# A hybrid decoder step with expert retrieval on one core: mixer steps of the second and third groups laid closer, VectorE without a slot's lag

## The reference

```
h1  = rmsnorm(x) * (1 + sc1) + sh1
proj = h1 @ w_in + b_in                 # 1024 -> 1536: pooling part, conv value, conv gate
pool_out = (window means over 2/4/8/16 rows - hp) @ w_pool * pool_scale
conv_out = silu(layernorm(depthwise causal conv, 31 taps, of cv * sigmoid(cg)))
x  = x + gt1 * (concat(pool_out, conv_out) @ w_out + b_out)
h2 = rmsnorm(x) * (1 + sc2) + sh2
q  = h2 @ w_query                       # 1024 -> 2048 (8 heads, 2 halves of 128)
s  = q . sub_keys                       # 128 scores for each head and half
16 best of each half -> 256 sums -> 16 best: eid (of 16384 experts), gate = softmax
a   = u_table[eid] . h2                 # 128 experts for each token
x  = x + gt2 * sum(gelu(a) * gate * v_table[eid]);   y = rmsnorm(x)
```

## Time and profile before

| what | value |
|---|---|
| median of 3 runs | 3502.99 us (3493.56 to 3516.3) |
| profiled execution, span from first to last instruction | 3289.1 us |
| median less span | 213.9 us |
| mean granted TensorE clock | 0.823 |
| instructions | 30699 |
| bytes moved by DMA | 1235.08 MB, mean 376 GB/s |

### The profile page before, as it was taken

The page is one execution under the profiler, slowest core; times in us unless marked ns, Lnnn a source line. Parts: engine busy times, 40 slices in busy tenths (PEclk is TensorE's granted clock), DMA queues, the critical chain, the costliest instruction groups (busy, mean ns, idle before and its releaser), DMA issues.

```text
span 3289.1 us, 30699 instructions
## 1 busy us (share of the span) xinstructions
PE 2159.5 (66%) x9831; PEld 958.8 (29%) x9831; DVE 2139.4 (65%) x4892; ACT 368.6 (11%) x793; POOL 2280.5 (69%) x2229
## 2 busy tenths in 40 slices
PE   6885896756776468997855577767454445545556
PEld 5573442212443113453211143434111111111111
DVE  1577756676788855666575657877766666677431
ACT  2112231100010110222100100001000000000000
POOL 0144677776777777777776777777777777777765
PEclk9997998977887789999877688889767777667679
DMA  8778899999999999999999999999999999999998
GB/s 290 202 273 299 326 385 386 388 401 401 397 395 389 360 396 406 405 405 386 382 400 394 375 399 390 392 382 370 369 405 406 402 402 406 406 385 402 382 363 321
DMA packets 363454, 1235.08 MB, mean 376 GB/s; under 512 B 36855, under 2 KB 40335, under 8 KB 363279
## 3 DMA queue, kind: packets, MB, share of 16 engines
q0 software_dynamic: 304784, 1109.40, 87.4%
q1 hardware_dynamic: 36335, 79.69, 6.8%
q10 hardware_dynamic: 22176, 44.04, 3.6%
HBM read 1220.31 MB, written 13.28 MB: 375 GB/s over the span
## 4 chain that ended last, share of the span: by engine, by line
POOL 29%; DMA 27%; PE 24%; issue 11%; DVE 7%; DVEq 1%; ACT 1%; SPq 0%; POOLq 0%; ACTq 0%
DMA v_ring<-in_v_table_dram,eidt 21%; POOL u_ring L807 15%; POOL v_ring L827 14%; PE bank L1758 13%; DMA u_ring<-in_u_table_dram,eid 4%; PE bank L1586 3%; PE bank L1668 2%; DVE u_ring L1381 2%; PE bank L1569 2%; PE bank L1644 2%; DMA u_ring<-in_v_table_dram,eidt 1%; DVE mixt L1211 1%; DVE work L1272 0%; DMA u_ring<-in_w_ada_dram 0%; POOL u_ring L827 0%
## 5 line engine op out<-in xcount | busy, mean ns | idle before, releaser
L1758 PE MATMUL bank<-v_ring,act_x 128*32 128x512 f32 x4104 | 1177.7, 808 | 977.7 <-DMA v_ring<-in_v_table_dram,eidt 929.9
L1381 DVE CUSTOM_DVE_ANT_0 u_ring<-u_ring,h 128x1024 f32<-128x1024 f32 x1056 | 1279.5, 1226 | 785.4 <-DMA u_ring<-in_u_table_dram,eid 711.9
L807 POOL DMA_INDIRECT u_ring<-in_u_table_dram,eid x1024 | 1129.9, 1103 | 444.0 <-issue 312.2
L827 POOL DMA_INDIRECT v_ring<-in_v_table_dram,eidt x1026 | 1070.3, 1043 | 397.3 <-issue 245.8
L1758 PEld LDWEIGHTS bank<-v_ring,act_x 128*32 128x32 f32 x4104 | 271.4, 135 | 1794.3 <-issue 1785.0
L1668 PEld LDWEIGHTS bank<-hbuf,wring 128*128 128x128 f32 x1984 | 228.4, 194 | 22.0 <-issue 22.0
L1668 PE MATMUL bank<-hbuf,wring 128*128 128x128 f32 (+1 forms) x1984 | 234.4, 279 | 0.0
L1586 PE MATMUL bank<-zc,dring 128*128 128x384 f32 x496 | 193.3, 514 | 4.0 <-ACT dring L860 4.0
L1569 PE MATMUL bank<-hbuf,wring 128*128 128x384 f32 (+2 forms) x448 | 150.8, 495 | 22.7 <-DMA wring<-in_w_in_dram 13.7
L1644 PE MATMUL bank<-wring,mixt 128*128 128x512 f32 (+1 forms) x256 | 123.2, 631 | 0.0
L1569 PEld LDWEIGHTS bank<-hbuf,wring 128*128 128x128 f32 x448 | 85.7, 194 | 89.7 <-issue 50.8
(11 more groups left out here) (267 smaller groups left out, 1696.6 us busy)
## 6 DMA issues: line engine op xcount, KB each, us to landing
v_ring<-in_v_table_dram,eidt POOLq DMA_INDIRECT x1026, 6.9
u_ring<-in_u_table_dram,eid POOLq DMA_INDIRECT x1024, 6.8
wring<-in_w_out_dram ACTq DMA_DIRECT2D x16, 1024.0 KB, 11.9
wring<-in_w_query_dram ACTq DMA_DIRECT2D x16, 1024.0 KB, 11.7
wring<-in_w_in_dram ACTq DMA_DIRECT2D x10, 1024.0 KB, 11.8
xr<-in_x_prompt_dram SPq DMA_DIRECT2D x16, 512.0 KB, 7.4
v_ring<-in_w_ada_dram SPq DMA_DIRECT2D x7, 1024.0 KB, 13.4
wring<-in_w_ada_dram SPq DMA_DIRECT2D x5, 1024.0 KB, 5.6
```

The costliest lines, as they stand in the source:

```text
L807: pool.indirect_dma_start(u_ring[:, n % NU], None, u_table[0], bass.IndirectOffsetOnAxis(ap=col, axis=0)).then_inc(u_in[n % NU], 16)
L827: pool.indirect_dma_start(place, None, v_table[0], bass.IndirectOffsetOnAxis(ap=eidt[:, b % RING, t:t + 1], axis=0)).then_inc(landed, 16)
L1381: dve.tensor_tensor_reduce(u_ring[:, n % NU], u_ring[:, n % NU], h2[:, b % 2], 1.0, 0.0, ALU.mult, ALU.add, dot[:, b % 2, k:k + 1]).then_i ...
L1758: last = pe.matmul(acc[h][j * S:(j + 1) * S, :], act_x[:, i % 2, j, a:a + S], v_place(n)[0][:, h * HALF:(h + 1) * HALF], start=(c == 0), s ...
```

## The change

`ROOM` becomes 8 for both groups; most gaps in `mixer_steps` shrink; `s` may follow `s` after one slot instead of two; both halves of `best` lie in the slot of their `s`; `turned` lies right behind its `turn`. VectorE does the steps of a slot in that very slot (`DVE_LAG` is gone). `finish` moves from the end of slot 17 of a row to its beginning, ahead of the dots; the store and load of y go from slot 20 to slot 18. Nothing is computed more or less.

Where the steps lie, from the two lists that `lay_out` gives:

| steps | slots before | slots after |
|---|---|---|
| second group: `xn`, `x` | 5 to 10 | 5 to 8 |
| `in` (24) | 10 to 16 | 8 to 14 |
| `conv` (16) | 16 to 27 | 14 to 23 |
| `pool` to `silu` | 28 to 36 | 23 to 26 |
| `out`, `add`, `norm`, `turn2` | 37 to 52 | 27 to 37 |
| `q` (24), `s`, `best` (12) | 53 to 78 | 38 to 53 |
| third group: `state`, `xn`, `x` | 77 to 85 | 53 to 58 |
| `in` (24) | 87 to 98 | 59 to 66 |
| `conv` (16) | 99 to 114 | 67 to 74, two in each |
| `pool` to `silu` | 115 to 120 | 75 to 77 |
| `out`, `add`, `norm`, `turn2` | 121 to 146 | 78 to 93 |
| `q` (32), `s`, `best` (16) | 147 to 184 | 94 to 114 |
| `state_out` | 183, 184 | 114 |
| last piece of block 8 | 251 | 249 |

The diff is long because it also brings code for a second way of doing the expert layer, over lists that are empty here: with `DENSE = []` there are no dense steps, `POS` is the identity, `NPP` is `NB`, `V_LAST` and `u_uses` give the same numbers as before, and `dots_before` is 0. What acts is this:

```diff
-ROOM = [None, 7, 4.6]
+ROOM = [None, 8, 8]
+DENSE = []
...
 def top_steps(todo):
-        out += [("turn", *h) for h in half] + [("top", *x, 3)] + [("turned", *h) for h in half] + [("top", *x, 4), ("top", *x, 5)]
+        out += [("turn", *h) for h in half] + [("turned", *h) for h in half] + [("top", *x, i) for i in (3, 4, 5)]
...
 def mixer_steps(g):
-        out += [("xn", b)] + ([("gap", 2)] if i else []) + [("x", a) for a in bs[i - 1:i]]
+        out += ([("gap", 1)] if i >= 2 else []) + [("xn", b)] + ([("gap", 1)] if i == 1 else []) + [("x", a) for a in bs[i - 1:i]]
...
-    out += [("mean", g), ("gap", 4 if g == 1 else 1), ("centre", g), ("gap", 1), ("square", g), ("gap", 1), ("var", g), ("gap", 1), ("silu", g), ("gap", 1)]
+    out += [("mean", g), ("gap", 1), ("centre", g), ("square", g), ("gap", 1), ("var", g), ("silu", g), ("gap", 1)]
...
-        for b in bl:
-            out += [("gap", 1 if b != SB else 3), ("add", b)]
-        for b in bl:
-            if b != SB:
-                out += [("gap", 1), ("norm", b)]
-        out += [("gap", 2)] + [("turn2", b) for b in bl if b != SB]
+        out += [("gap", 1)] + [("add", b) for b in bl if b != SB]
+        out += [("gap", 2), ("add", SB)] if SB in bl else []
+        out += [("gap", 1)] + [("norm", b) for b in bl if b != SB]
+        out += [("gap", 1)] + [("turn2", b) for b in bl if b != SB]
...
 def lay_out():
             if i[0] == "s":
-                at = max(at, scored.get("last", 0) + 2)
+                at = max(at, scored.get("last", 0) + 1)
...
-                scored["last"], scored[i[1:]] = at, at + 1
+                scored["last"], scored[i[1:]] = at, at
                 for h in range(2):
-                    slots[at + h].append(("best", *i[1:], h))
+                    slots[at].append(("best", *i[1:], h))
...
 # VectorE
-                    if p < NB or c < NSG:
-                        chunk(p, c)
-                    slot = p * NCH + c - DVE_LAG
-                    for step in steps[slot] if slot >= 0 else []:
+                    for end in ends[p * NCH + c]:
+                        finish(end)
+                    for j in range(CH):
+                        if p < NPP or c < NSG:
+                            dots(p, c, j, j + 1)
+                    dve.drain()
+                    for step in steps[p * NCH + c]:
...
-                    if p and c == V_LAG:
-                        finish(p - 1)
...
 # SyncE
-                if s % NCH == V_LAG + 3 and 0 < p < NB:
-                    y_store(p - 1)
-                    y_load(p)
+                for end in ends[s - 1] if s else []:
+                    y_store(f)
+                    if f < NB - 1:
+                        y_load(f + 1)
```

More of the change, by code:

```diff
@@ L161, in lay_out @@
 def lay_out():
-    slots = [[] for _ in range((NB + 1) * NCH)]
+    slots = [[] for _ in range(NSLOT)]
     load = [0] * len(slots)
@@ L418, in build @@
+        ud_in = [sem(f"ud_in{i}") for i in range(NUD)]
+        vd_in = [sem(f"vd_in{i}") for i in range(NVD)]
+        ut_ps, ut_ready, a_ps, ge_ready, wd_ready, vd_ps, dacc_free = (
+            sem(n) for n in ("ut_ps", "ut_ready", "a_ps", "ge_ready", "wd_ready", "vd_ps", "dacc_free"))
         steps = lay_out()
-        DVE_LAG = 1
+        dense, dense_ends = lay_out_dense(steps)
+        ends, END_ORDER = lay_out_ends(dense_ends)
+        END_NO = {x: i for i, x in enumerate(END_ORDER)}
+        END_BLOCK = [POS[x[1]] if x[0] == "row" else DENSE[x[1]][x[2]] for x in END_ORDER]
@@ L421, in build, with dots_before, turns_before @@
         SPREAD_AT = (0, 1)
-        turned = [sum(1 for s_ in range(V_LAG + LAG * i) for step in steps[s_] if step[0] == "turn") for i in range(2 * NB)]
-        turned.append(2 * NB + 1)
+        def dots_before(s):
+            return sum(1 for todo in dense[:s] for x in todo if x[0] == "round" and 0 <= x[2] - NDB - 1 < NKEY)
+        def turns_before(s):
+            return sum(1 for todo in steps[:s] for x in todo if x[0] == "turn")
+        turned = [sum(1 for s_ in range(V_LAG + LAG * i) for step in steps[s_] if step[0] == "turn") for i in range(2 * NPP)]
@@ L495, in build @@
         XNO = {use: i for i, use in enumerate(XUSE)}
-        transfers = [[] for _ in range((NB + 1) * NCH)]
+        transfers = [[] for _ in range(NSLOT)]
         for s_, todo in enumerate(steps):
@@ new lines, in dense_transfers @@
+            def dense_transfers(*step):
+                kind, r = step[:2]
+                if kind == "numbers" and step[2] == 0:
+                    for t in range(3):
+                        ud_load(r, t)
+                elif kind == "unit":
+                    u = step[2]
+                    if u and u % (STOK // UNIT) == 0:
+                        stage_store(r, u // (STOK // UNIT) - 1)
+                elif kind == "last":
+                    stage_store(r, NSTAGE - 1)
+                elif kind == "round":
+                    m = step[2]
+                    if m + 3 < NTILE:
+                        ud_load(r, m + 3)
+                    if m == 0:
+                        g_load(r, 0)
+                        g_load(r, 1)
+                    elif m % IC == IC - 3 and m // IC + 1 in range(2, NCHUNK):
+                        g_load(r, m // IC + 1)
+                    if 0 <= m - 1 < NKEY:
+                        vd_load(r, m - 1)
@@ L996, in next_tile, with dense_step @@
+            def dense_step(*step):
+                if step[0] == "numbers":
+                    gates_taken(*step[1:])
+                elif step[0] == "unit":
+                    second_keys(*step[1:])
+                elif step[0] == "last":
+                    unit_out(step[1], NUNIT - 1)
+                else:
+                    dense_round(*step[1:])
             def next_tile(*used):
@@ new lines, in dense_dots @@
+            def dense_dots(r, i, s):
+                n = r * NKEY + i
+                pe.wait_ge(act_taken, halves(s))
+                pe.wait_ge(eidt_ready, turns_before(s))
+                pe.wait_ge(ut_ready, 2 * (r * NTILE + NDB + i + 1))
+                if n:
+                    pe.wait_ge(ge_ready, n)
+                for k in range(KC):
+                    last = pe.matmul(ps[6][:, DT:2 * DT], ut[i % 2][:, k * P:(k + 1) * P], ht[:, k, :], start=(k == 0), stop=(k == KC - 1))
+                last.then_inc(a_ps, 1)
```

496 lines of the change are left out of this document (406 added, 90 removed).

## The result

Slower, and by three times what was predicted: **3778.06 us** (median of 4 runs, 3772.37 to 3784.46) against 3498.27 (4 runs, 3483.65 to 3516.3). The ratio is 1.078, with a 95% interval from 1.0733 to 1.0827: +280 us where +90 was forecast.

The account below looks back on a forecast made before the run. Transfers were taken to bound the kernel from slot 17 on. The terms 10 + 7 + 22 + 35 + 16 + 15 - 15 gave +90 us on 3503, so 3593 us, range 3455 to 3690.

Parts of the forecast that it names:

- step 8: VectorE without its lag: nothing less computed, priced in the query and third-group stages; bounds 0 and +140 us.
- step 3: Second group's queries, 16 slots: VectorE becomes the bound, 222 us in all; +22 us (+7 to +35).
- Steps 1 to 5: The mixer stages repriced in packed slots, freed slots at 10.68 us each: +10, +7, +22, +35 and +16 us.
- Steps 3 and 5: Both groups' query stages, with VectorE's own work as bound: +22 us (+7 to +35) and +16 us (+1 to +32).
- Step 4: Third group up to h2, 40 slots: eight TensorE-bound conv slots at 15.8 us; +35 us.
- Steps 2 and 5: Second group's layer norm to h2, +7 us; third group's queries, +16 us (+1 to +32).
- much slower: Rival: each `best` slot becomes a chain across engines, 5 us in 28 slots; sum +230, 3733 us; chance 0.12.
- Step 6: `turned` in the slot of its `turn`: free in calm slots, 3 to 5 us in each of five packed slots; +15 us.
- Step 7: `finish` ahead of the dots: TensorE's 42.2 us wait for the release of banks shrinks; -15 us (-42 to 0).
- The two tests of the last paragraph: Conv slots at 15 to 16 us, TensorE over 95% busy; query slots at 13 to 15 us, VectorE over 90%.
- The level: The median of the runs lay 213.9 us above the profiled span; this was carried over unchanged.
- The bounds: The forecaster's own case ran from 3540 to 3680 us, by the bounds of both query stages and the `finish` move.

Follow-up runs that it names:

- after_2: The kernel after, unchanged, timed again beside the kernel before: 3765.77 us, 1.0803.
- lag_back_2: Second run of the kernel after with VectorE one slot behind again, packing kept: 3621.77 us, 1.0379; the first run took 3644.23 us, 1.0402.
- before_again: The kernel before, unchanged, timed and profiled again: 3505.11 us, 0.9999.
- b_nolag: The kernel before with its own layout, VectorE's steps in their own slot and `finish` ahead of the dots: 3706.69 us, 1.0565.
- b_room8: The kernel before with only `ROOM = [None, 8, 8]`, lag kept: 3344.11 us, 1.0151; run again, 3561.0 us, 1.0183.

## Why the prediction was wrong

The sign was right; **step 8 failed**, which gave the missing lag of VectorE no price of its own. In the set that holds both (`after_2`, `lag_back_2`, before at 3488.14) the change cost 278 us: 144 of them are the lag, and all the rest, with the lag in place, cost 134 for a sum of 90, half as much again. The steps against the traces, each as the stretch after, plus 11.75 us for each slot that it gave up, less the stretch of `before_again`:

| step | predicted | lag put back | after |
|---|---|---|---|
| 1 projection and conv, second group | +10 | +16 | +18 |
| 2 layer norm to h2 | +7 | +19 | +12 |
| 3 queries, second group | +22 | +27 | +69 |
| 4 third group up to h2 | +35 | +35 | +61 |
| 5 queries, third group | +16 | +29 | +77 |
| slots 115 to 263 | (in 6) | -11 | +7 |
| sum | +90 | +115 | +244 |

For instance step 3: 285.5 + 9 x 11.75 - 322.7 = 68.6 after, 243.5 + 9 x 11.75 - 322.7 = 26.6 with the lag. The sums stand against 245.8 and 112.0 us between the spans; the small differences lie in slots 0 to 7 and the tail.

- *Steps 1 to 5* came to +126 for +90 with the lag in place. Steps 3 and 5 lie inside their ranges (up to +35 and +32), near the upper ends: a mean of 15.2 and 14.9 us a slot, so the rings evened out less than the middle that I took. Their mechanism, VectorE's own work as the bound, is not borne out: it was busy 75 and 73% of these stretches with the lag, 65 and 64% without. Step 4 was right to the microsecond by the sum, but by luck: the conv slots took 14.4 with the lag (TensorE 98% busy, as foreseen) for my 15.8, and the slots around them more. Steps 2 and 5, at +19 for +7 and +29 for +16, were missed most.
- *Step 8*, "nothing less is computed ... I price this in 3, 5 and 6", with bounds of 0 and +140, took nearly the lower end. It is worth 134 us on the new layout (`lag_back` against after, 144 when both were run again) and some 200 on the old (`b_nolag`). The evidence used against the chain, that the fetches of one more slot are under way, is true and not enough: the ring holds a slot and a half of fetches, some 18 us at 11.75 a slot, and in the timeline above VectorE stood 24 us. The sum itself was made of each engine's work in a slot, and a wait between two engines in the same slot is in no engine's work. The rival "much slower" had the chain link by link and its 5 us a slot; measured are (42 + 48) / 28 = 3.2 us in each `best` slot, and 44 us more in slots 54 to 93 and 115 to 263, where the rival booked nothing.
- *Step 6*, +15. VectorE's wait for the bank of `turn` (lines 1639, 2039) is 108.8 us in eight waits of after and 38.9 in five with the lag. The size of the wait was missed; what it costs by itself I did not measure. In slots 54 to 93 it is 61.0 us in two waits against 23.0 in two.
- *Step 7*, -15. TensorE's wait on the release of the banks fell from 26.6 us to 10.3, as foretold, but VectorE now waits for TensorE in `finish`, a wait that the step did not count: before the last row it stands 1.7 us in all in `before_again` and 38 in after. Slots 16 to 18 of seven rows took 313.7 us with the lag and 348.6 in after against 290.9. I never ran it alone, so that it gains nothing is an inference.
- *The two tests of the last paragraph.* Conv slots at 16.2 us, clock 0.99 and 276 GB/s: met, but for a length just above 16 and TensorE's 93% instead of 95. `best` slots at 13 to 15 us with VectorE over 90%: not met, 17.8 and 17.2 with VectorE at 65%; the sign of the chain that I had set at 18 us was all but reached. POOL over 100 us for the dots: met, 385; TensorE under 20 for the release of the banks: met, 10.3. The calm slots were 11.8 us instead of 10.7, in both kernels alike.
- *The level.* "I carry that over unchanged" put 213.9 us outside the span. They lay inside it, in slower slots from slot 17 on: of the 237 us between the two spans of the kernel before 84 are in the calm slots, and 149 in slots 17 to 184. This did not cause the miss: the differences came out the same at either level (`b_room8` 1.015 and 1.018), except that taking the lag away without the scores' meeting cost 1.8% at the lower and 3.1% at the upper.
- *The bounds.* "3540 to 3680 by the bounds of 3, 5 and 7" does not follow: these three reach from 3536 to 3637. Even 3680 lies 98 us below the result.

That VectorE's lag guarded the kernel is shown, by putting it back on the new layout. That the wait for the scores is half of what the lag and the place of `finish` are worth on the old layout is shown too; on the new one it is argued from the waits. There it is not alone: in the two query stretches TensorE also stood 22.9 and 21.5 us for `weigh`, 2.6 and none with the lag. The loss in slots 54 to 93 (+26 us, after against lag put back) cannot be the scores, since no `s` lies there; the row that grew is the wait for the bank of `turn`. No run takes out either of these two meetings alone, and the other half of the loss on the old layout stays open.

## What to carry to other kernels

When engines run through common slots, look for each slot at the longest chain across engines, not only at the busiest engine; a stage of lag between producer and consumer costs nothing in work and was worth about 4% here, and on the looser layout up to 6% together with the place of `finish`. Before pricing a change on a profile, hold its span against the timed runs: if they differ, profile again and find the stretches that differ (here all from slot 17 on) before anything is said to be "outside". And when a step is moved closer, look at what its consumer will do in the same slot, and which fetch is queued behind that consumer.

## What the runs showed of the hardware

The same kernel took 3296.5 us (13 runs, 3288.83 to 3308.18) on one chip and 3485 to 3509 on four others (medians, one set of runs on each, so what the chip does and what the hour does is not parted). With it goes the rate of the gathers: 402 GB/s in slots 185 to 263 of `b_room8`, 365 in `b_room8_2`, the same kernel:

```profile
2392.60:3226.20 833.60, 432.51 (x1301) 99.52 (x1301) 531.02 (x1046) 35.87 (x66) 629.68 (x633) 0.70 1.02 402
```

```profile
2521.80:3439.90 918.10, 443.78 (x1301) 97.57 (x1301) 530.21 (x1048) 35.88 (x66) 656.55 (x632) 0.69 0.96 365
```

833.6 against 918.1 us for 79 slots, 10.55 and 11.62 each, while VectorE's busy time is the same to 1 us and the granted clock to 0.01. The DMA share is 1.02 and 0.96: the engines of the slower one are not even fuller. What makes it I do not know. It is not TensorE's clock: 16 more matmuls a slot raised that, and the time rose by 0 to 1%.
